# Sixteen small read-back transfers per scan step, issued by ScalarE instead of SyncE

## The chip, the cores and the metric

One core of one Trainium2 chip runs the whole program. The metric is the device time in microseconds (us) from the first to the last instruction of the core. One program computes two transformer-like blocks one after the other; the change is in one stage of the first block, the scan, which takes from about 624 us to 1393 us of the profiled execution.

## The reference, cut to what matters

The scan stage computes a linear recurrence over a 64x64 state per head, for 8 heads, in two directions (forwards and backwards), over 256 context tokens and then 1024 sequence tokens:

```python
def wkv_scan(state0, r, decay, kk, b, v, k, reverse):
    def step(S, inp):
        r_t, w_t, kk_t, b_t, v_t, k_t = inp
        sa = jnp.einsum("bhvk,bhk->bhv", S, kk_t)
        S = (S * w_t[:, :, None, :] - sa[..., None] * b_t[:, :, None, :]
             + v_t[..., None] * k_t[:, :, None, :])
        return S, jnp.einsum("bhvk,bhk->bhv", S, r_t)
    ...
    S, ys = lax.scan(step, state0, xs, reverse=reverse)
```

Everything else (projections, convolution, feed-forward block, two kinds of attention) runs before or after the scan and is not touched.

## The kernel before, in words

**Chunks.** The recurrence is done in chunks of 64 tokens: 4 chunks of context and 16 of sequence make `STEPS` = 20 steps, and each step handles one chunk of both directions x = 0 and x = 1, with all 8 heads held as 4 pairs. Within a chunk, the rank-one updates need the inverse of a 64x64 triangular matrix per head. It is put together from the inverses of its two 32x32 diagonal blocks: `level_y` and `last_u` on TensorE join them into the full inverse `uend`.

**The block inverses.** VectorE computes the 32x32 inverses for four steps at a time (`BATCH` = 4), spread over 128 partitions, in three parts that lie at the ends of steps s with s % 4 = 0, 1, 2 (`blocks(T, part)`). Part 2 ends with the semaphore `ui`. GpSimd then writes a transposed copy (`turned`, semaphore `ti`), and SyncE stores both to DRAM (`store_blocks`, semaphores `ub` and `tb`). From DRAM they come back in the layout of a step: `load_inverse(u)` waits, for the first step of a batch, until both stores have landed, and issues sixteen transfers of 16 KB (two directions x two heads of a pair x two blocks x two tensors `ud` and `td`), which raise the semaphore `inv`. `level_y(u)` on TensorE waits for it.

**The order of the queues.** Each engine's order is written out by hand. In step s:

- SyncE (the DMA queue SP): `load_inverse(s + 2)` unless s + 2 starts a batch; the stores of `raw` (s % 4 < 2, until step 9); the load of `nb` for the next batch of inverses (steps 1, 5, 9), which waits for part 1 of VectorE (`w_last`); the loads of `pre` (s % 4 >= 2, until step 7); then `load(x, s + 2)` for both directions, six transfers each (`rk`, `vc`, `kbk` and `vd` twice), which wait for the last reader of the buffers, `p_y` of the same direction (`p_s` in the first four steps); then the stores of `yo` to `ys`; and in steps with s % 4 = 2 `store_blocks` and then `load_inverse(s + 2)`.
- TensorE: `token_major(s + 1)` (line 1035, the transposes, which wait for the loads of step s + 1), `chain_g`, `triangles` l (bank 0, after ScalarE has copied `bet` out of it), `chain_z`, `triangles` m, `chain_s`, `level_y(s + 1)`, `chain_y`, `last_u(s + 1)`. Nearly all of it is in the helper `heads`, line 1005.
- ScalarE (helper `copy`, line 1136): four copies `c_bk` of `token_major(s + 1)`, two `c_gg`, two `c_zc`, the four half copies `c_zd`, where there are blocks the copies `c_raw`, and two `c_yo`, in this order.

So an engine that waits holds up everything behind it in this list. In the traces below the lines of the transfers are 889 to 894 (`load`), 900 (`load_pre`), 912 (`store_raw`), 921 (`load_blocks`), 925 and 927 (`store_blocks`), 942 and 944 (`load_inverse`) and 967 (`ys`).

Of the kernel before, what the change touches and what calls it, by code (L numbers as in the profile page):

```python
# [25 lines left out]
HEAD = 64  # L26
CH = 512
PAIRS = CH // P
# [5 lines left out]
STEPS = NCTX + NSEQ  # L34
# [788 lines left out]
def scan(nc, d, t):  # L823

    DIRS, HEADS = range(2), range(2)
    ROWS = [slice(HEAD * h, HEAD * h + HEAD) for h in HEADS]
    LOADS = 6 * 16
    BATCH = 4
    NBATCH = STEPS // BATCH
    HB = C // 2  # L830
    with ExitStack() as st:
# [46 lines left out]
        @block.sync  # L878
        def _(sp):
            def wait(name, x, value):  # L880
                if value > 0:
                    sp.wait_ge(S(name, x), value)

            def load(x, s):
                par, slot = s % 2, slot_of(x, s)
                ld_ = S(f"loaded{par}_", x)
                at = slice(slot * C, slot * C + C)
                part = lambda a0, a1, rows: d["ops"][x, a0:a1, :, rows, at].rearrange("a q p c -> p (a q) c")
                sp.dma_start(rk[x][par][:].rearrange("p a q c -> p (a q) c"), part(0, 2, slice(0, P))).then_inc(ld_, 16)
                sp.dma_start(vc[x][par][:], d["vts"][slot]).then_inc(ld_, 16)  # L890
                for h, rows in enumerate(ROWS):
                    sp.dma_start(kbk[x][par][rows, :, :, h].rearrange("p a q c -> p (a q) c"),
                                 part(1, 4, rows)).then_inc(ld_, 16)
                    sp.dma_start(vd[x][par][rows, :, h], d["vts"][slot, rows]).then_inc(ld_, 16)

            def load_pre(i):
                for x in DIRS:
                    wait("p_pre", x, i - 1)
                    slot = min(slot_of(x, 2 * i), slot_of(x, 2 * i + 1))
                    sp.dma_start(pre[x][i % 2][:].rearrange("p a q c -> p (a q) c"),  # L900
                                 d["ops"][x, 1:3, :, :, slot * C:(slot + 2) * C].rearrange("a q p c -> p (a q) c")
                                 ).then_inc(S(f"pre{i % 2}_", x), 16)

            def store_raw(i):

                for x in DIRS:
                    wait("raw", x, i + 1)
                    for h in HEADS:
                        for b in range(2):
                            rows = slice(HEAD * h + HB * b, HEAD * h + HB * (b + 1))  # L910
                            n = i % 2 * 2 * PAIRS
                            sp.dma_start(d["pb"][i // 2, x, h, b, n:n + 2 * PAIRS].rearrange("n r c -> r n c"),
                                         raw[x][i % 2][rows, :, :, HB * b:HB * (b + 1)].rearrange("p j q c -> p (j q) c")
                                         ).then_inc(sem(f"pb{i % 2}"), 16)

            def load_blocks(T):
                for j in range(2):
                    sp.wait_ge(sem(f"pb{j}"), 128 * (T + 1))
                if T:
                    sp.wait_ge(sem("w_last"), T)  # L920
                sp.dma_start(nb[:, 0:HB * HB], d["pb"][T].rearrange("x h b n r c -> (x h b n) (r c)")).then_inc(sem("nb"), 16)

            def store_blocks(T):
                sp.wait_ge(sem("ui"), T + 1)
                sp.dma_start(d["ub"][T].rearrange("x h b n r c -> (x h b n) (r c)"), ui[:, 0:HB * HB]).then_inc(sem("ub"), 16)
                sp.wait_ge(sem("ti"), T + 1)
                sp.dma_start(d["tb"][T].rearrange("x h b n r c -> (x h b n) (r c)"), ti[:].rearrange("p r c -> p (r c)")).then_inc(sem("tb"), 16)

            def load_inverse(u):
                T, par = u // BATCH, u % 2  # L930
                if u % BATCH == 0:
                    sp.wait_ge(sem("ub"), 16 * (T + 1))
                    sp.wait_ge(sem("tb"), 16 * (T + 1))
                for x in DIRS:
                    wait("uend", x, u - 1)
                    j = u % BATCH if x == 0 else u % BATCH // 2 * 2 + 1 - u % 2
                    of_u, of_t = (d["ub"], d["tb"]) if x == 0 else (d["tb"], d["ub"])
                    for h in HEADS:
                        for b in range(2):
                            rows, at = slice(HEAD * h + HB * b, HEAD * h + HB * (b + 1)), slice(HB * b, HB * (b + 1))  # L940
                            n = slice(PAIRS * j, PAIRS * (j + 1))
                            sp.dma_start(ud[x][par][rows, :, h, at], of_u[T, x, h, b, n].rearrange("n r c -> r n c")
                                         ).then_inc(S(f"inv{par}_", x), 16)
                            sp.dma_start(td[x][par][rows, :, at], of_t[T, x, h, b, n].rearrange("n r c -> r n c")
                                         ).then_inc(S(f"inv{par}_", x), 16)

            def step(s):
                if s + 2 < STEPS and (s + 2) % BATCH:
                    load_inverse(s + 2)
                if has_pre(s):  # L950
                    store_raw(pre_at(s))
                if s % BATCH == 1 and s // BATCH + 2 < NBATCH:
                    load_blocks(s // BATCH + 2)
                if s % BATCH >= 2 and s // BATCH + 3 < NBATCH:
                    load_pre(2 * (s // BATCH + 3) + s % BATCH - 2)
                for x in DIRS:
                    if s + 2 < STEPS:

                        if has_y(s):
                            wait("p_y", x, s + 1 - NCTX)  # L960
                        else:
                            wait("p_s", x, s + 1)
                        load(x, s + 2)
                for x in DIRS if has_y(s) else ():
                    wait("yo", x, s + 1 - NCTX)
                    at = slot_of(x, s) * C
                    sp.dma_start(d["ys"][x, :, :, at:at + C].rearrange("q p c -> p q c"),
                                 yo[x][s % 2][:]).then_inc(S(f"stored{s % 2}_", x), 16)
                if s % BATCH == 2 and s + 2 < STEPS:
                    store_blocks((s + 2) // BATCH)  # L970
                    load_inverse(s + 2)

            for i in range(2):
                load_pre(i)
            for par in range(2):
                for x in DIRS:
                    sp.wait_ge(sem("zeros"), 2 * par + x + 1)
                    load(x, par)
            for i in range(2):
                store_raw(i)  # L980
            load_pre(2)
            load_blocks(0)
            load_pre(3)
            for i in (2, 3):
                store_raw(i)
            load_pre(4)
            load_pre(5)
            load_blocks(1)
            sp.wait_ge(sem("clear"), 1)
            store_blocks(0)  # L990
            load_inverse(0)
            load_inverse(1)
            for s in range(STEPS):
                step(s)
            for x in DIRS:
                for par in range(2):
                    sp.wait_ge(S(f"stored{par}_", x), 16 * (NSEQ // 2))
# [132 lines left out]
        def _(act):  # L1130
# [4 lines left out]
            def copy(out, src, scale=1.0):  # L1135
                return nc.scalar.activation(out, src, ACT.Copy, scale=scale)

            def blocks(x, i):
                wait("p_pre", x, i + 1)
                if i >= 2:  # L1140
                    act.wait_ge(sem(f"pb{i % 2}"), 128 * (i // 2))
                copy(raw[x][i % 2][:].rearrange("p j q c -> p (j q c)"), bank[x][3][:]).then_inc(S("raw", x), 1)
# [33 lines left out]
            for i in (2, 3):  # L1176
                for x in DIRS:
                    blocks(x, i)
            for s in range(STEPS):
                if s + 1 < STEPS:  # L1180
                    token_major(s + 1)
                for x in DIRS:
                    chain_g(x, s)
                for x in DIRS:
                    chain_z(x, s)
                if has_y(s):
                    for x in DIRS:
                        chain_zd(x, s)
                if has_pre(s):
                    for x in DIRS:  # L1190
                        blocks(x, pre_at(s))
                if has_y(s):
                    for x in DIRS:
                        chain_y(x, s)

        @block.vector
        def _(dve):
# [1617 lines left out]
```

## Time and profile before

| what | value |
|---|---|
| median of 3 runs | 3318.89 us (3318.15 to 3340.68) |
| the profiled execution's own time | 3321.0 us |
| its span, first to last instruction | 3319.2 us |
| PE, DVE, ACT, POOL busy in the span | 2753.3, 1478.0, 812.2, 618.1 us |
| granted TensorE clock, share of full speed | 0.88 |
| scan, 624 to 1393 us: PE busy | 556.4 of 769 us |
| scan: granted clock, DMA share | 0.79, 0.37 |

PE is TensorE, DVE is VectorE, ACT is ScalarE, POOL is GpSimd; SPq and ACTq are the DMA queues of SyncE and ScalarE. The clock is a mean over the stretch. The DMA share is the mean busy share of the core's 16 DMA engines. Durations of an issue (SPq, ACTq) are the time that the issuing engine spends on it, not the transfer's.

### The profile page before, as it was taken

How to read it: one execution, taken by the hardware profiler on the slowest of the kernel's cores; microseconds unless marked ns; L12 is line 12 of the kernel's file. 1: busy time of each engine (PE TensorE's matmuls, PEld its weight loads, DVE VectorE, ACT ScalarE, POOL GpSimd, SP SyncE). 2: the span in 40 equal slices, each digit the busy share in tenths (PEclk: the TensorE clock that was granted, in tenths of full speed). 3: DMA queues.
4: the chain of work that ended last, by engine and by line, in shares of the span. 5: the costliest groups of instructions: out<-in, count | busy, mean ns of one | idle time of the engine just before them, and what ended most of it. 6: DMA issues, size and time to landing. Idle time of an engine off the chain costs nothing. (4 is left out here: it accounts for less than half of the span.)

```text
span 3319.2 us, 41107 instructions
## 1 busy us (share of the span) xinstructions
PE 2753.3 (83%) x14544; PEld 2303.8 (69%) x14544; DVE 1478.0 (45%) x1936; ACT 812.2 (24%) x1147; POOL 618.1 (19%) x302
## 2 busy tenths in 40 slices
PE   7788889747767888778799999697959898998879
PEld 6666668646766788756678888486747777776757
DVE  3166661254344353263466666402163554545251
ACT  1233321011111111133232333212232232223120
POOL 0334331000110101131222222233232011000001
PEclk8898888767878788889899999799979999998879
DMA  4233333433342424330111211423112101100022
GB/s 188 68 126 131 132 121 108 134 93 83 78 109 64 99 55 102 106 126 25 51 61 72 76 73 60 169 100 128 63 48 90 45 13 44 44 32 1 6 113 96
DMA packets 305065, 276.40 MB, mean 83 GB/s; under 512 B 228920, under 2 KB 264376, under 8 KB 293824
## 3 DMA queue, kind: packets, MB, share of 16 engines
q1 hardware_dynamic: 302656, 258.18, 24.3%
q10 hardware_dynamic: 2304, 16.78, 1.5%
q8 instruction: 70, 1.15, 0.1%
q14 instruction: 35, 0.29, 0.0%
HBM read 209.86 MB, written 65.04 MB: 83 GB/s over the span
## 5 line engine op out<-in xcount | busy, mean ns | idle before, releaser
L106 PE MATMUL e_ps<-h_hi,e_w_hi 128*128 128x512 f32 x704 | 276.6, 393 | 31.0 <-POOL e_w_lo L1935 30.2
L1959 DVE SCALAR_TENSOR_TENSOR e_acc<-e_grid,vec,e_acc 128x1024 f32<-128x1024 f32 x176 | 266.2, 1512 | 42.8 <-DVE e_acc L1959 37.4
L106 PE MATMUL e_ps<-h_hi,e_w_lo 128*128 128x512 f32 x704 | 274.8, 390 | 0.0
L106 PE MATMUL e_ps<-h_lo,e_w_hi 128*128 128x512 f32 x704 | 274.7, 390 | 0.0
L106 PE MATMUL b_ps<-h_hi,b_w_hi 128*128 128x512 f32 (+1 forms) x488 | 202.1, 414 | 39.1 <-POOL b_w_lo L651 31.6
L1035 PE MATMUL c_ps<-con,c_kbk 128*128 128x128 f32 x320 | 69.6, 390 | 153.4 <-DMA c_vd<-vts 153.4
L106 PE MATMUL b_ps<-h_lo,b_w_hi 128*128 128x512 f32 (+1 forms) x488 | 194.5, 399 | 0.0
L106 PE MATMUL b_ps<-h_hi,b_w_lo 128*128 128x512 f32 (+1 forms) x488 | 193.4, 396 | 0.0
L2063 PE MATMUL f_ps<-f_z_hi,f_w_hi 128*128 128x512 f32 x352 | 141.7, 403 | 49.2 <-DVE f_z_lo L2111 40.3
L1935 POOL TENSOR_TENSOR e_w_lo<-raw_up,e_w_hi 128x1024 fp32r<-128x1024 f32 x44 | 108.1, 2457 | 380.2 <-ACT e_w_hi L1906 380.2
L106 PEld LDWEIGHTS e_ps<-h_hi,e_w_hi 128*128 128x128 f32 x704 | 132.6, 188 | 66.1 <-issue 39.2
L1035 PEld LDWEIGHTS c_ps<-con,c_kbk 128*128 128x128 f32 x320 | 56.6, 204 | 162.3 <-DMA c_vd<-vts 162.3
L2419 POOL TENSOR_TENSOR g_w_lo<-raw,g_w_hi 128x1024 fp32r<-128x1024 f32 x32 | 76.6, 2406 | 474.9 <-ACT g_w_hi L2337 474.9
L106 PE MATMUL g_pb<-h_hi,g_w_hi 128*128 128x512 f32 x352 | 144.7, 411 | 9.7 <-issue 6.5
L106 PEld LDWEIGHTS b_ps<-h_hi,b_w_hi 128*128 128x128 f32 x488 | 100.2, 205 | 75.6 <-issue 56.6
L106 PEld LDWEIGHTS e_ps<-h_hi,e_w_lo 128*128 128x128 f32 x704 | 132.6, 188 | 27.9
L106 PEld LDWEIGHTS e_ps<-h_lo,e_w_hi 128*128 128x128 f32 x704 | 132.7, 189 | 27.0
L2265 PE MATMUL g_ps<-g_vt,g_pt 128*128 128x64 f32 x864 | 122.3, 292 | 30.1 <-DVE g_ot L2513 23.5
L1375 POOL TENSOR_SCALAR c_sd<-c_sc,con 128x256 f32<-128x256 f32 x64 | 58.4, 924 | 461.3 <-PE c_ps L1005 450.4
L106 PE MATMUL g_pb<-h_lo,g_w_hi 128*128 128x512 f32 x352 | 141.7, 402 | 0.0
L106 PE MATMUL g_pb<-h_hi,g_w_lo 128*128 128x512 f32 x352 | 141.6, 402 | 0.0
L2265 PEld LDWEIGHTS g_ps<-g_vt,g_pt 128*128 128x128 f32 x864 | 116.4, 211 | 36.2 <-issue 36.0
(320 smaller groups left out, 6232.7 us busy)
## 6 DMA issues: line engine op xcount, KB each, us to landing
raw_up<-w_ffn SPq DMA_DIRECT2D x22, 1024.0 KB, 4.9
raw_down<-w_down SPq DMA_DIRECT2D x16, 1408.0 KB, 6.1
b_adaw<-ada ACTq DMA_DIRECT2D x16, 1024.0 KB, 4.9
ops<-b_ops SPq DMA_DIRECT2D x16, 1024.0 KB, 4.5
raw<-w SPq DMA_DIRECT2D x8, 2048.0 KB, 7.6
c_kbk<-ops SPq DMA_DIRECT2D x80, 192.0 KB, 3.3
raw_in<-w SPq DMA_DIRECT2D x26, 512.0 KB, 3.8
zs<-e_z SPq DMA_DIRECT2D x22, 512.0 KB, 2.6
```

What stands on the lines that cost most here:

```text
L106: last = nc.tensor.matmul(out, w[:, k, :], x[:, k, cols], start=(k == 0 and n == 0), stop=(k == nk - 1 and n == 2))
L1035: mm = nc.tensor.transpose(bank[x][a][:, P * q:P * (q + 1)], kbk[x][par][:, 1 + a, q].rearrange("p h c -> p (h c)"), t["c_ident"])
L1375: a = TS(sd[x][:, :, h], sc[x][:], t["c_headones"][:, HEAD * h:HEAD * h + 1], None, ALU.mult)
L1935: nc.gpsimd.tensor_tensor(w_lo[:, s], raw[:, s], w_hi[:, s].bitcast(F32), ALU.subtract).then_inc(sem(f"lo{s}"), 1)
L1959: a = nc.vector.scalar_tensor_tensor(out=acc[:], in0=view, scalar=wt, in1=acc[:], op0=ALU.mult, op1=ALU.add)
L2063: mm = nc.tensor.matmul(ps[s][:], w[:, s, k], y[:, k], start=(k == 0 and n == 0), stop=(k == NFF - 1 and n == 2))
L2265: mm = nc.tensor.matmul(ps[0][:, 0:HEAD], pt[:, u % 2, b], vt[:, b, HEAD * h:HEAD * (h + 1)], start=(b == 0), stop=(b == qt))
L2419: nc.gpsimd.tensor_tensor(w_lo[:, tl], raw[:, tl], w_hi[:, tl].bitcast(F32), ALU.subtract).then_inc(sem(f"lo{tl}"), 1)
```

## The change: what it does

`load_inverse` moves from SyncE to ScalarE, unchanged in its waits, its transfers and its semaphores. ScalarE calls it for steps 0 and 1 ahead of its loop, and for step s + 2 as the last thing of its step s, behind the copies `c_yo`. SyncE keeps all the rest, `store_blocks` too.

```diff
@@ SyncE @@
-            def load_inverse(u):
-                T, par = u // BATCH, u % 2
-                if u % BATCH == 0:
-                    sp.wait_ge(sem("ub"), 16 * (T + 1))
-                    sp.wait_ge(sem("tb"), 16 * (T + 1))
...
             def step(s):
-                if s + 2 < STEPS and (s + 2) % BATCH:
-                    load_inverse(s + 2)
                 if has_pre(s):
                     store_raw(pre_at(s))
...
                 if s % BATCH == 2 and s + 2 < STEPS:
                     store_blocks((s + 2) // BATCH)
-                    load_inverse(s + 2)
...
             store_blocks(0)
-            load_inverse(0)
-            load_inverse(1)
             for s in range(STEPS):
                 step(s)
@@ ScalarE @@
+            def load_inverse(u):
+                T, par = u // BATCH, u % 2
+                if u % BATCH == 0:
+                    act.wait_ge(sem("ub"), 16 * (T + 1))
+                    act.wait_ge(sem("tb"), 16 * (T + 1))
+                for x in DIRS:
+                    wait("uend", x, u - 1)
+                    j = u % BATCH if x == 0 else u % BATCH // 2 * 2 + 1 - u % 2
+                    of_u, of_t = (d["ub"], d["tb"]) if x == 0 else (d["tb"], d["ub"])
+                    for h in HEADS:
+                        for b in range(2):
+                            rows, at = slice(HEAD * h + HB * b, HEAD * h + HB * (b + 1)), slice(HB * b, HB * (b + 1))
+                            n = slice(PAIRS * j, PAIRS * (j + 1))
+                            nc.scalar.dma_start(ud[x][par][rows, :, h, at], of_u[T, x, h, b, n].rearrange("n r c -> r n c")
+                                         ).then_inc(S(f"inv{par}_", x), 16)
+                            nc.scalar.dma_start(td[x][par][rows, :, at], of_t[T, x, h, b, n].rearrange("n r c -> r n c")
+                                         ).then_inc(S(f"inv{par}_", x), 16)
...
+            act.wait_ge(sem("clear"), 1)
+            load_inverse(0)
+            load_inverse(1)
             for s in range(STEPS):
                 if s + 1 < STEPS:
                     token_major(s + 1)
...
                 if has_y(s):
                     for x in DIRS:
                         chain_y(x, s)
+                if s + 2 < STEPS:
+                    load_inverse(s + 2)
```

## Rows read from the trace of the kernel before

**Rows 1.** Groups of instructions, 637 to 1393 us: busy, mean ns | idle before, releaser

```profile
L1035 PE MATMUL c_ps<-con,c_kbk 128*128 128x128 f32 x320 | 69.6, 390 | 153.4 <-DMA c_vd<-vts 153.4
```

**Rows 2.** Timeline of SyncE's queue, step 16: start us, duration us, what

```profile
1297.15 0.43 SPq L944 DMA_DIRECT2D c_td<-ub  x1
1309.50 0.39 SPq L889 DMA_DIRECT2D c_rk<-ops  x1
1316.72 0.65 SPq L894 DMA_DIRECT2D c_vd<-vts  x1
```

**Rows 3.** Timeline of ScalarE, steps 16 and 17, the last column is idle before

```profile
1298.78 0.38 ACT L1136 ACTIVATE c_zc<-c_ps 128x256 f32<-128x256 f32 x1 [2.30 <-PE c_ps L1005]
1309.50 0.38 ACT L1136 ACTIVATE c_yo<-c_ps 128x256 f32<-128x256 f32 x1 [7.71 <-PE c_ps L1005]
1312.18 0.38 ACT L1136 ACTIVATE c_yo<-c_ps 128x256 f32<-128x256 f32 x1 [2.30 <-PE c_ps L1005]
1320.78 0.60 ACT L1136 ACTIVATE c_bk<-c_ps 128x512 f32<-128x512 f32 x1 [3.76 <-PE c_ps L1035]
1324.65 0.38 ACT L1136 ACTIVATE c_gg<-c_ps 128x256 f32<-128x256 f32 x1 [1.56 <-PE c_ps L1005]
1329.11 0.38 ACT L1136 ACTIVATE c_zc<-c_ps 128x256 f32<-128x256 f32 x1 [2.30 <-PE c_ps L1005]
```

**Rows 4.** Stretches: us, engines' busy time (count), granted clock, DMA share, GB/s

```profile
1311.40:1319.40 8.00, 3.24 (x27) 2.81 (x26) 1.37 (x2) 0.98 (x2) 1.88 (x3) 1.00 0.96 229
1128.00:1133.00 5.00, 5.00 (x47) 5.00 (x46) 2.80 (x6) 2.05 (x5) 0.00 (x0) 1.00 0.23 34
```

**Rows 5.** Timeline of SyncE's queue, steps 6 and 7

```profile
973.18 0.32 SPq L942 DMA_DIRECT2D c_ud<-ub  x1
...
981.34 0.44 SPq L942 DMA_DIRECT2D c_ud<-ub  x1
...
990.03 1.02 SPq L889 DMA_DIRECT2D c_rk<-ops  x1
```

**Rows 6.** Timeline of ScalarE, steps 6 to 8

```profile
956.85 0.38 ACT L1136 ACTIVATE c_yo<-c_ps 128x256 f32<-128x256 f32 x1 [2.30 <-PE c_ps L1005]
...
974.38 0.38 ACT L1136 ACTIVATE c_zc<-c_ps 128x256 f32<-128x256 f32 x1 [2.30 <-PE c_ps L1005]
...
1003.49 0.60 ACT L1136 ACTIVATE c_bk<-c_ps 128x512 f32<-128x512 f32 x1 [3.82 <-PE c_ps L1035]
```

**Rows 7.** Timeline of TensorE, step 7: triangles l, then chain_z

```profile
971.50 2.00 PE L1005 MATMUL c_ps<-c_rk,c_kbk 128*128 128x128 f32 x16
973.34 1.90 PE L1005 MATMUL c_ps<-c_gg,c_uend 128*128 128x64 f32 x16
```

**Rows 8.** Timeline of SyncE's queue, step 3: first transfer of the batch's second step

```profile
830.99 0.43 SPq L942 DMA_DIRECT2D c_ud<-ub  x1
```

**Rows 9.** Timeline of ScalarE, steps 2 to 4

```profile
786.73 0.60 ACT L1136 ACTIVATE c_bk<-c_ps 128x512 f32<-128x512 f32 x1 [3.17 <-PE c_ps L1035]
...
799.07 0.38 ACT L1136 ACTIVATE c_zc<-c_ps 128x256 f32<-128x256 f32 x1 [3.52 <-PE c_ps L1005]
...
814.35 1.09 ACT L1136 ACTIVATE c_bk<-c_ps 128x512 f32<-128x512 f32 x2 [3.30 <-PE c_ps L1035]
...
826.31 0.38 ACT L1136 ACTIVATE c_zc<-c_ps 128x256 f32<-128x256 f32 x1 [3.58 <-PE c_ps L1005]
...
852.99 0.60 ACT L1136 ACTIVATE c_bk<-c_ps 128x512 f32<-128x512 f32 x1 [3.47 <-PE c_ps L1035]
```

**Rows 10.** Stretches, as rows 4, each just after a long wait of TensorE

```profile
787.00:800.00 13.00, 13.00 (x73) 13.00 (x72) 2.04 (x4) 2.71 (x7) 0.00 (x0) 0.59 0.15 45
935.00:943.00 8.00, 8.00 (x63) 8.00 (x62) 1.29 (x3) 2.56 (x5) 0.00 (x0) 0.84 0.36 108
```

**Rows 11.** Timeline of both DMA queues, 498 us, an issue on each at once

```profile
498.18 0.34 SPq L334 DMA_DIRECT2D mixd<-b_r  x1
498.42 0.34 ACTq L547 DMA_DIRECT2D b_adaw<-ada  x1
```

More of the change, by code:

```diff
@@ L927, in store_blocks @@
                 sp.dma_start(d["tb"][T].rearrange("x h b n r c -> (x h b n) (r c)"), ti[:].rearrange("p r c -> p (r c)")).then_inc(sem("tb"), 16)
-            def load_inverse(u):
-                T, par = u // BATCH, u % 2
-                if u % BATCH == 0:
-                    sp.wait_ge(sem("ub"), 16 * (T + 1))
-                    sp.wait_ge(sem("tb"), 16 * (T + 1))
[L934 to L945, printed above, removed]
             def step(s):
-                if s + 2 < STEPS and (s + 2) % BATCH:
-                    load_inverse(s + 2)
                 if has_pre(s):
```

## The prediction

> **What bounds the kernel now.** I read the groups of instructions of the scan first: which group is TensorE idle in front of? It is the transposes on line 1035, which open a step, with 153.4 us of idle time released by the loads of the step's inputs [rows 1]. So every scan step is a chain through SyncE's queue, and the next view is that queue's timeline in an ordinary step, beside ScalarE's. In step 16 the last of the sixteen inverse transfers is issued at 1297.15, and then the queue is idle until the loads start at 1309.50 [rows 2], the moment in which ScalarE is also released by the same `p_y` [rows 3]. The sixteen issues are therefore finished 12 us before the loads become possible: **in an ordinary step they delay nothing where they are**. The twelve loads are issued until 1316.72 + 0.65 = 1317.37 [rows 2], and the second direction's `c_bk` copy runs at 1320.78 [rows 3]. Third, the stretches: from 1311.4 to 1319.4 the DMA engines are 0.96 busy [rows 4], so in that window the transfers themselves are the limit, not only their issue.
>
> The exception is the turn of a batch (steps 2, 6, 10 and 14 and the step after each). There the queue waits for the stores, issues 32 inverse transfers (973.18 on, the second sixteen from 981.34) and only then, at 990.03, the loads [rows 5]. That step is long.
>
> **What goes.** The time from direction 0's `c_zc` to direction 1's next `c_bk` is 1320.78 - 1298.78 = 22.0 in the ordinary step [rows 3]. At the turn it is 1003.49 - 974.38 = 29.1 [rows 6]. With the queue free and the first batch of transfers landed early this falls to the ordinary length: 7.1 us less, in each of three turns of this pattern (6, 10, 14). In the first turn the steps have no output: 852.99 - 826.31 = 26.7 against the preceding step's 814.35 - 799.07 = 15.3 [rows 9], 11.4 less. Together 3 x 7.1 + 11.4 = **-32.7**.
>
> **What comes, first: ScalarE stalls at the turns.** ScalarE's last copy of step 6 ends at 957.23 [rows 6]. Behind it now stand the waits for both stores, which let SyncE go at 973.18, and sixteen issues, 973.18 to 981.34 = 8.2 us with SyncE's own durations [rows 5]; an issue alone costs ScalarE's queue the same as SyncE's, 0.34 [rows 11]. SyncE has issued that step's loads before, so nothing disturbs this batch. Queued behind it on ScalarE are the four `c_bk` and the `c_gg` copies of step 7; TensorE waits for them in `triangles` and `chain_z`. From 981.34: four copies of 0.60 [rows 3] are 2.4, `c_gg` 0.38, then from `chain_z`'s start to `c_zc` 974.38 - 973.34 = 1.04 [rows 6, 7]; the triangles, 973.34 - 971.50 = 1.84 [rows 7] after the first copy, fit beside that. So `c_zc` comes at 981.34 + 3.8 = 985.2 instead of 974.38: +10.8. In the first turn it is 830.99 + 3.8 = 834.8 instead of 826.31 [rows 8, 9]: +8.5. Together 3 x 10.8 + 8.5 = **+40.9**. `level_y` comes after that and finds its transfers landed. The POOL queue and `store_blocks` are passed by nothing: they stand where they were.
>
> **Second: ordinary steps, on ScalarE.** Its issues start when the second `c_yo` ends, 1312.18 + 0.38 = 1312.56, and take 8.2 at most: 1320.7. The first `c_bk` is late by that, but the second was only due at 1320.78 and the first `c_gg` at 1324.65 [rows 3]; four copies from 1320.7 end at 1323.1. Cost **0**; the cover is the wait for the loads itself, with 1.5 us to spare. Were the issues slower by more than that, each microsecond more would be paid in every step. In the first four steps, without `c_yo`, they start earlier still.
>
> **Third: ordinary steps, on the DMA engines.** Before, the sixteen transfers ran while the engines were idle; now they run from 1312.6 on, inside the full window. Alone they take 0.23 of the engines [rows 4] for some 8.2 x 0.23 = 1.9 us of their time; those issued before the last load lands are about four fifths, 1.5 us, and in a window that is full that much work pushes the last load back by as much. No row shows what the engines do between two queues. From below: 0, if the loads' backlog is served first. From above: the issues hinder each other (first rival), 3.5. I take 1.5, since the 0.96 row is the nearest. It counts in eleven steps: 18 have a `load_inverse`, less four turns, less steps 1, 5 and 9, in which SyncE still waits for VectorE when ScalarE has finished. 11 x 1.5 = **+16.5**.
>
> Here the Trainium skill speaks against the change. Its page "DMA: Bandwidth & Descriptors", section "Queues, rings and completion order", says that an engine takes turns between the queues that have work for it. By it the small transfers aren't held back behind the loads, and all sixteen count, 1.9 us in each step in place of 1.5: 4 us more in the sum. No row of before has both queues full, so the trace neither agrees nor disagrees.
>
> **Fourth: the clock.** A new wait of some 10 us in `triangles` (from about 971.5 to 982) comes at each turn. After long waits TensorE restarts at the lower clock: it was granted 0.59 over 13 us in one case and 0.84 over 8 us in another [rows 10]. At the low clock the way from `c_bk` to `c_zc` took 799.07 - 786.73 = 12.3 [rows 9], in step 17 1329.11 - 1320.78 = 8.3 [rows 3]: 4.0 dearer. Per turn 0 to 4, I take 2: 4 x 2 = **+8**. The eleven steps wait 1.5 us longer too; if one in ten of them falls to the long low stretch it is 11 x 0.4 = **+4.4** (0 to 11).
>
> **The sum.** -32.7 + 40.9 + 0 + 16.5 + 8 + 4.4 = +37.1. The profiled execution took 3321.0, 2.1 above the median of the runs shown; against it the sum gives 3358.1, against the median 3318.9 + 37.1 = **3356**. The transfers for steps 0 and 1, ahead of the loop, stand behind the same stores on either queue: nothing.
>
> **Rivals.**
> - *The issues of the two queues exclude each other.* After 1312.56 SyncE has 4.8 us of its twelve issues left, seven loads; if each lets one inverse issue through, 8.2 / 16 = 0.5, the last load goes 3.5 us later. That replaces the 1.5 (the backlog then drains meanwhile): 11 x 2.0 = +22, so 3378. For it: issues back to back take longer than one alone (0.65 against 0.39 [rows 2]), so something behind the queue is occupied. Against: two issues that overlapped by 0.1 us took 0.34 each [rows 11], but both were alone in their queue. The Trainium skill, "Perfetto Trace Analysis", section "DMA Instruction — HWDGE (DVE, Sync)", says that the descriptor generator is locked for one issue at a time; by that rule this rival holds.
> - *The loads aren't disturbed.* SyncE's backlog is served first, both clock terms small: -32.7 + 40.9 = +8.2, plus at most 5, so 3327 to 3332. For it: five loads are issued before ScalarE starts. Against: the 0.96.
> - *Faster, by the turns.* The price of the stall is decided in ScalarE's step after a turn: if its copies didn't have to wait for the end of the issues (the stores early, or the step's copies already done), only -32.7 + 16.5 remains, 3303, and 3286 without the disturbance as well. It decides from a stall under 7.1 us per turn. Against: ScalarE would have to be released by 977.6 instead of 981.34, and its first issue can't start before 973.18.
> - *It doesn't do what it says*: nothing is reordered by the change beyond these queues; a gain or loss within 3 us either way would need all four terms to cancel.
>
> **How the numbers follow.** About 1%, 33 us, is what a measurement of this kernel tells from no change, so the limits are 3286 and 3352. Forecast case 0.50, lying at 3340 to 3372 by the clock and the stall's length, so six tenths of it above 3352; exclusion 0.25 (3365 to 3395); undisturbed 0.17; faster 0.05, half of it past 3286; no effect 0.03. Slower 0.30 + 0.25 = 0.55 and a little of the third's upper end, 0.57; faster 0.03; the same 0.40. The range takes the undisturbed case and the bulk of the exclusion: 3326 to 3390.
>
> **What would show it.** ScalarE idle from about 957 to 973 at the turn and its sixteen issues behind, TensorE waiting some 10 us before `triangles` l there, released by `c_bk`; the turn's second half 7 us shorter, with the loads issued at `p_y`; in ordinary steps `p_y` to the second direction's transposes 1.5 us longer, the DMA share near 1.0 over a longer stretch, and SyncE's issues of 0.65 as they were (in the first rival they grow to over 1 us). Wrong if ScalarE's issues cost over 0.6 each, if the loads land no later, or if TensorE's clock in the scan moves from 0.79 by more than 0.03.

## The result, and the profile after

After: 3348.54 us median of 19 runs (3332.84 to 3367.23). Before, on the same chip: 3318.15 (19 runs, 3301.34 to 3340.68). The ratio is 1.0096, 95% interval 1.0075 to 1.0117: some 30 us slower, at the limit of 1%. The forecast was +37.

The profiled execution of after took 3332.84 us, the lowest of the 19, so its span is only 12 us longer than before's. From direction 0's `c_zc` of step 0 to that of step 19, though, it is 676.5 us against 659.5: +17.0. Ahead of it +5.5 and behind it -10.6 are work that the change doesn't touch (5.3 of the 5.5 are there already at the last `c_raw` copy before the scan steps, 673.72 against 668.43, and TensorE's wait for the two batches ahead of the loop is the same, 34.4 against 34.5 us).

In after, `heads` is line 982 (1005 before), the transposes 1012 (1035), ScalarE's copy 1113 (1136), the moved transfers 1128 and 1130 (942, 944). From the page: busy time by engine, the clock by slice, the queues (packets, MB, share).

```profile
PE 2722.4 (82%) x14544; PEld 2273.1 (68%) x14544; DVE 1475.9 (44%) x1936; ACT 809.9 (24%) x1147; POOL 629.1 (19%) x302
PEclk8798888867878788979899999899979999999989
q1 hardware_dynamic: 256576, 252.92, 23.2%
q10 hardware_dynamic: 48384, 22.04, 2.5%
```

ScalarE's queue q10 now carries the transfers (2304 packets before, 48384 now). Work and clock did not become worse in this execution: PE is busy 30.9 us less, at 0.885 of full speed against 0.880. The loss is waiting. Where, the groups of the scan show (637 to 1410 us; columns as in [rows 1]):

```profile
L982 PE MATMUL c_ps<-c_rk,c_kbk 128*128 128x128 f32 x640 | 88.5, 297 | 43.0 <-ACT c_bk L1113 43.0
L1012 PE MATMUL c_ps<-con,c_kbk 128*128 128x128 f32 x320 | 70.8, 396 | 154.3 <-DMA c_vd<-vts 154.3
L1113 ACT ACTIVATE c_bk<-c_ps 128x512 f32<-128x512 f32 x80 | 45.6, 598 | 341.8 <-issue 180.8 <-PE c_ps L1012 160.9
```

The wait for the loads is as in [rows 1] (154.3, 153.4). New is the first line: `triangles` waits 43.0 us for `c_bk`, and waited 0.0 before. The third says why `c_bk` is late: for over half of the idle time before it ScalarE waited for nothing that is computed ("issue"), but was with its own queue. At a turn, where [rows 6] stood, ScalarE's timeline of steps 6 to 8 is:

```profile
962.17 0.38 ACT L1113 ACTIVATE c_yo<-c_ps 128x256 f32<-128x256 f32 x1 [2.30 <-PE c_ps L982]
979.29 0.31 ACTq L1128 DMA_DIRECT2D c_ud<-ub  x1
...
986.40 0.45 ACTq L1130 DMA_DIRECT2D c_td<-ub  x1
986.90 2.06 ACT L1113 ACTIVATE c_bk<-c_ps 128x512 f32<-128x512 f32 x4 [24.35 <-issue]
...
991.90 0.38 ACT L1113 ACTIVATE c_zc<-c_ps 128x256 f32<-128x256 f32 x1 [2.39 <-PE c_ps L982]
...
1014.29 1.71 ACT L1113 ACTIVATE c_bk<-c_ps 128x512 f32<-128x512 f32 x3 [8.61 <-issue]
```

Four `c_bk` back to back are a pile that waited: 24.35 us idle, which end with the last of sixteen issues. TensorE, transposes and then `triangles` l and `chain_z` of step 7 [rows 7]:

```profile
970.34 2.82 PE L1012 MATMUL c_ps<-con,c_kbk 128*128 128x128 f32 x12 [3.98 <-DMA c_vd<-vts]
...
987.55 3.48 PE L982 MATMUL c_ps<-c_rk,c_kbk 128*128 128x128 f32 x16 [10.65 <-ACT c_bk L1113]
990.86 1.90 PE L982 MATMUL c_ps<-c_gg,c_uend 128*128 128x64 f32 x16
```

And SyncE's queue, which at 981.34 was in the middle of 32 issues [rows 5], is idle until `p_y` releases its loads:

```profile
973.84 0.33 SPq L925 DMA_DIRECT2D ub<-c_ui  x1
975.84 0.33 SPq L927 DMA_DIRECT2D tb<-c_ti  x1
976.21 1.47 SPq L900 DMA_DIRECT2D c_pre<-ops  x2
1002.62 0.37 SPq L889 DMA_DIRECT2D c_rk<-ops  x1
```

In an ordinary step, 15 to 16, first SyncE, then ScalarE, then TensorE, where [rows 2, 3] stood:

```profile
1299.42 0.38 SPq L889 DMA_DIRECT2D c_rk<-ops  x1
...
1301.83 0.98 SPq L892 DMA_DIRECT2D c_kbk<-ops  x1
...
1307.04 0.65 SPq L894 DMA_DIRECT2D c_vd<-vts  x1
```

```profile
1302.11 0.39 ACT L1113 ACTIVATE c_yo<-c_ps 128x256 f32<-128x256 f32 x1 [2.29 <-PE c_ps L982]
1302.12 0.33 ACTq L1128 DMA_DIRECT2D c_ud<-ub  x1
...
1310.56 0.45 ACTq L1130 DMA_DIRECT2D c_td<-ub  x1
1311.06 0.60 ACT L1113 ACTIVATE c_bk<-c_ps 128x512 f32<-128x512 f32 x1 [8.56 <-issue]
1311.83 0.60 ACT L1113 ACTIVATE c_bk<-c_ps 128x512 f32<-128x512 f32 x1 [0.17 <-PE c_ps L1012]
...
1315.96 0.38 ACT L1113 ACTIVATE c_gg<-c_ps 128x256 f32<-128x256 f32 x1 [1.83 <-PE c_ps L982]
```

```profile
1310.67 2.82 PE L1012 MATMUL c_ps<-con,c_kbk 128*128 128x128 f32 x12 [3.88 <-DMA c_vd<-vts]
```

The second `c_bk` is released by PE, not by "issue": ScalarE was ready 0.17 us before it was needed.

The ledger, from the `c_zc` of direction 0 in the two traces (us; a turn is two steps; `c_yo` is that of direction 0 in the step before):

| turn | length before | after | `c_yo` to `c_zc` before, after | `c_zc` to 2nd `c_bk` before, after |
|---|---|---|---|---|
| steps 3, 4 | 62.3 | 65.2 | (step length 27.24, 38.89) | 26.7, 17.9 |
| 7, 8 | 68.3 | 74.5 | 20.2, 32.4 | 29.1, 22.9 |
| 11, 12 | 70.6 | 74.8 | 20.1, 32.1 | 27.0, 23.3 |
| 15, 16 | 65.7 | 74.5 | 20.0, 32.0 | 27.9, 23.1 |

The first halves cost 11.6 + 12.2 + 12.0 + 12.0 = 47.9 (from the unrounded lengths), the second give back 8.8 + 6.2 + 3.8 + 4.7 = 23.5. The turns together are 22.1 longer; in before, step 12 had a low-clock stretch between its `c_bk` and `c_zc` (below), so it is some 26 with that set aside.

What the second half gives back has two sources, and only one is SyncE's shorter queue. In before, TensorE also waits at the turns inside `level_y`, for direction 1's transfers, and each time a stretch at the low clock follows (0.50 to 0.53 of full speed). In step 15 of before, then the same place in step 7 of after, where `c_zc` is so late that all sixteen have landed:

```profile
1272.72 1.94 PE L1005 MATMUL c_ps<-c_td,c_ld 128*128 128x64 f32 x8 [1.76 <-DMA c_td<-ub]
1273.00:1279.00 6.00, 6.00 (x30) 6.00 (x29) 0.69 (x1) 0.00 (x0) 0.00 (x0) 0.50 0.23 35
```

```profile
997.96 1.95 PE L982 MATMUL c_ps<-c_td,c_ld 128*128 128x64 f32 x16
```

From `c_zc` to the next `c_yo` before took 13.1, 14.6 and 16.0 us in steps 7, 11 and 15; after takes 10.7 each time, 11.5 less together. In steps 11 and 15 that is the whole give-back: from `c_yo` to the second `c_bk` of the next step it is 12.4 and 11.9 us before, 12.5 and 12.4 after. Only step 7 (16.1 to 12.2) and the first turn, which has no `c_yo`, are shorter by the loads.

### The profile page after: what moved, and what is told of

It reads as the page before. It is cut to its first block and busy times, and to the rows that moved or that the text cites. A ratio compares the mean times of both kernels' runs of the same rounds, so it can differ in the third digit from the quotient of the medians.

```text
span 3331.1 us, 41107 instructions
## 1 busy us (share of the span) xinstructions
PE 2722.4 (82%) x14544; PEld 2273.1 (68%) x14544; DVE 1475.9 (44%) x1936; ACT 809.9 (24%) x1147; POOL 629.1 (19%) x302
## 3 DMA queue, kind: packets, MB, share of 16 engines
q10 hardware_dynamic: 48384, 22.04, 2.5%
## 5 line engine op out<-in xcount | busy, mean ns | idle before, releaser
L106 PE MATMUL e_ps<-h_hi,e_w_hi 128*128 128x512 f32 x704 | 275.7, 392 | 32.4 <-POOL e_w_lo L1935 32.4
L1959 DVE SCALAR_TENSOR_TENSOR e_acc<-e_grid,vec,e_acc 128x1024 f32<-128x1024 f32 x176 | 264.2, 1501 | 42.8 <-DVE e_acc L1959 37.4
L1012 PE MATMUL c_ps<-con,c_kbk 128*128 128x128 f32 x320 | 70.8, 396 | 154.3 <-DMA c_vd<-vts 154.3
L1935 POOL TENSOR_TENSOR e_w_lo<-raw_up,e_w_hi 128x1024 fp32r<-128x1024 f32 x44 | 118.8, 2700 | 368.4 <-ACT e_w_hi L1906 368.4
L106 PEld LDWEIGHTS e_ps<-h_hi,e_w_hi 128*128 128x128 f32 x704 | 132.7, 188 | 65.3 <-issue 37.1
L2265 PE MATMUL g_ps<-g_vt,g_pt 128*128 128x64 f32 x864 | 114.6, 280 | 32.2 <-DVE g_ot L2513 25.8
L2063 PE MATMUL f_ps<-f_z_lo,f_w_hi 128*128 128x512 f32 x352 | 140.5, 399 | 0.0
```

The costliest lines, as they stand in the source:

```text
L106: last = nc.tensor.matmul(out, w[:, k, :], x[:, k, cols], start=(k == 0 and n == 0), stop=(k == nk - 1 and n == 2))
L1012: mm = nc.tensor.transpose(bank[x][a][:, P * q:P * (q + 1)], kbk[x][par][:, 1 + a, q].rearrange("p h c -> p (h c)"), t["c_ident"])
L1935: nc.gpsimd.tensor_tensor(w_lo[:, s], raw[:, s], w_hi[:, s].bitcast(F32), ALU.subtract).then_inc(sem(f"lo{s}"), 1)
L1959: a = nc.vector.scalar_tensor_tensor(out=acc[:], in0=view, scalar=wt, in1=acc[:], op0=ALU.mult, op1=ALU.add)
L2063: mm = nc.tensor.matmul(ps[s][:], w[:, s, k], y[:, k], start=(k == 0 and n == 0), stop=(k == NFF - 1 and n == 2))
L2265: mm = nc.tensor.matmul(ps[0][:, 0:HEAD], pt[:, u % 2, b], vt[:, b, HEAD * h:HEAD * (h + 1)], start=(b == 0), stop=(b == qt))
```

## The experiments

All ratios are against runs of the kernel before on the same chip. The diffs are against after or before as said. In `e1_turns`, `e2_ordinary`, `e4_mid` and `e5_second` one engine issues the first batch of four steps and the other the second, so the second waits for both stores as well (`u % BATCH < 2` in place of `== 0`); the diffs leave this line and the copied `load_inverse` out.

**Where the loss sits: turns alone, the rest alone.** `e1_turns`, against after: ScalarE issues only the batches that open four steps; SyncE issues all others where it did before.

```diff
 (ScalarE)
-                if s + 2 < STEPS:
+                if s + 2 < STEPS and (s + 2) % BATCH == 0:
                     load_inverse(s + 2)
 (SyncE)
+                if s + 2 < STEPS and (s + 2) % BATCH:
+                    load_inverse(s + 2)
```

> ScalarE issues only the four batches that open a turn (steps 4, 8, 12 and 16), at the end of its step; all others stay on SyncE. Theory (the loss is ScalarE's stall at the turns, some 12 us each, less what SyncE's shorter queue gives back there): most of the loss is still there, 15 to 25 us over the kernel before, ratio 1.005 to 1.008, and from direction 0's c_yo to the next second c_bk in ordinary steps it is 11.8 as before, not 12.5. Rival (the loss is the clash with the loads in ordinary steps): within 5 us of the kernel before.

Measured: 3348.34 us, 1.0073 (1.0048 to 1.0098). `c_yo` to `c_zc` at the turns is 31.9 to 32.4, as in after; the second transposes of steps 9, 13, 14, 17 and 18 start 10.7 us after `c_yo`, near before's 10.6. `e2_ordinary` is the reverse (SyncE keeps the opening batches, ScalarE issues all others at the end of its step).

> The reverse: SyncE keeps the four batches that open a turn, ScalarE issues all others at the end of its step. Theory: no stall at the turns (c_bk at its old place, 4 us after c_yo), so the kernel is no slower than the one before: +8 us for the clash in eleven steps (0.7 each), -10 to -20 at the turns because SyncE issues 16 instead of 32 before the loads; ratio 0.996 to 1.001. Rival (clash in ordinary steps carries the loss): +15 us or more, ratio 1.005 or over.

Measured: 3320.73 us, 0.9986 (0.9964 to 1.0008). No loss. So the loss is made where ScalarE waits for the stores and issues sixteen in one go; what the other fourteen batches cost and what they give back at the turns come out even here. 1.0096 - 1.0073 = 0.0023, 8 us, is what they add in after, if the difference of two ratios, each uncertain by as much, is taken at its word.

**What of the stall is the wait, what the issues.** `e8_wait`, against before: ScalarE only waits, and issues nothing.

```diff
+                if s % BATCH == 2 and s + 2 < STEPS:
+                    act.wait_ge(sem("ub"), 16 * ((s + 2) // BATCH + 1))
+                    act.wait_ge(sem("tb"), 16 * ((s + 2) // BATCH + 1))
```

> The kernel before, all transfers on SyncE, but ScalarE also waits for both stores at the end of steps 2, 6, 10 and 14. It pays the wait and not the sixteen issues. Theory: the stall in the changed kernel is the wait (some 4 us beyond its cover) and the issues (7.6 us), one after the other; here only the first: direction 0's c_zc 24 to 25 us after the preceding c_yo instead of 20.1 (changed kernel: 32.1), and a part of it hidden since level_y waits for its transfers anyway; +6 to +14 us over the kernel before. Rival (the wait alone makes the loss): as slow as the kernel with the turns on ScalarE, +25.

Measured: 3319.99 us, 1.0017 (0.9998 to 1.0035), by the ratio 5.6 us and just under the 6 to 14 expected. ScalarE at the turn:

```profile
973.86 2.06 ACT L1136 ACTIVATE c_bk<-c_ps 128x512 f32<-128x512 f32 x4 [15.97 <-DMA tb<-c_ti]
...
978.85 0.38 ACT L1136 ACTIVATE c_zc<-c_ps 128x256 f32<-128x256 f32 x1 [2.38 <-PE c_ps L1005]
```

`c_zc` comes 3.8 us late (24.0 after `c_yo`, against 20.2), but steps 7 and 8 together take 68.5 us, as before (68.3). What comes behind was waiting for SyncE anyway and now waits less: `c_yo` of step 7 to the second `c_bk` of step 8 is 13.1 us (16.1 before), and `c_zc` to `c_yo` in steps 11 and 15 is 10.8 and 12.8 (14.6 and 16.0). The issues behind the wait are what costs.

`e10_half`, against before: ScalarE issues only direction 1's eight transfers of the opening batch at the end of its step; SyncE keeps direction 0's.

```diff
-            def load_inverse(u):
+            def load_inverse(u, dirs=DIRS):
...
-                for x in DIRS:
+                for x in dirs:
 (SyncE, s % BATCH == 2)
-                    load_inverse(s + 2)
+                    load_inverse(s + 2, (0,))
 (ScalarE, end of the step)
+                if s % BATCH == 2 and s + 2 < STEPS:
+                    load_inverse(s + 2, (1,))
```

> The kernel before, but of the batch that opens a turn ScalarE issues direction 1's eight transfers, at the end of steps 2, 6, 10 and 14; direction 0's eight and all else stay on SyncE. The stall now holds eight issues. Theory (the stall lengthens by each issue, 0.48 us): the preceding c_yo to direction 0's c_zc is 28 us at the turns, between 24.0 with none and 32.1 with sixteen; 5 to 15 us over the kernel before. Rival (what follows the wait is paid once, not per issue): 32.

Measured: 3338.63 us, 1.0042 (1.0016 to 1.0067). `c_yo` to `c_zc` is 28.6, 28.7 and 28.9 at the three turns. With the wait alone, eight issues and sixteen it is 24.0, 28.7 and 32.2: 4.7 for the first eight, 3.5 for the next. The stall grows with the number of issues ahead of `c_bk`.

**The price of one issue.** `e3_tiny`, against after: each of the moved transfers brings one partition instead of 32, so the step's inverses are incomplete.

```diff
-    nc.scalar.dma_start(ud[x][par][rows, :, h, at], of_u[T, x, h, b, n].rearrange("n r c -> r n c")
+    nc.scalar.dma_start(ud[x][par][rows.start:rows.start + 1, :, h, at], of_u[T, x, h, b, n, 0:1].rearrange("n r c -> r n c")
```

> The changed kernel with the same sixteen issues, each carrying one of its 32 partitions (so the inverses are mostly left out and the output is not the reference's). If the 0.7 us by which loads land later in ordinary steps is the DMA engines' work, it goes: c_yo to second c_bk back to 11.8, time 5 to 10 us under the changed kernel's 3348. If the two queues' issues exclude each other it stays at 12.5, and SyncE's load issues stay as long as in the changed kernel. The stall at the turns stays in both.

Measured: 3368.97 us, 1.0131 (1.0092 to 1.017): slower, against expectation. The bytes of a transfer fell to a thirty-second, but its issue became dearer:

```profile
981.14 0.56 ACTq L1128 DMA_DIRECT2D c_ud<-ub  x1
...
989.97 0.56 ACTq L1130 DMA_DIRECT2D c_td<-ub  x1
990.58 2.06 ACT L1113 ACTIVATE c_bk<-c_ps 128x512 f32<-128x512 f32 x4 [26.10 <-issue]
```

0.56 us each against 0.45 makes 9.4 us for sixteen, 1.8 more, and the way from there to `c_zc` is longer too: `c_yo` to `c_zc` at the turns is 34.5 to 35 us. The turn steps 3, 7, 11 and 15 are 1.0, 2.5, 2.4 and 2.7 us longer than in after, 8.7 together, most of the 0.0035 between the two ratios: the loss grows with the time of an issue, not with the bytes. In the ordinary steps ScalarE is busy until 12.5 us after `c_yo` (11.7 in after), later than its second `c_bk` is wanted, and still nothing is paid in the steps at the high clock: steps 13, 14 and 18 take 31.40, 30.61 and 31.11 us, in after 31.50, 30.70 and 31.23, for the first `c_gg` is on time (15.42 us after `c_yo` in step 14, 15.52 in after). The cover is the time to the first `c_gg`, as the prediction had it, and not to the second `c_bk`. (Steps 8, 16 and 17 of this run fell into low-clock stretches and those of after didn't; such stretches vary by as much in one kernel, see `e6_again`, so that this has to do with the longer burst is not shown.) The second transposes start at 10.8 us after `c_yo` on the mean of steps 9, 13, 14, 17 and 18 (11.1 in after, 10.6 before). The run was meant to isolate the clash on the DMA engines through `c_bk`, and `c_bk` here is set by ScalarE: for that it was the wrong measure.

**The rest of the gain, without the loss.** `e4_mid`, against before: SyncE keeps the opening batches, ScalarE issues all others in the middle of its step, ahead of the `c_yo` copies.

```diff
 (SyncE)
-                if s + 2 < STEPS and (s + 2) % BATCH:
-                    load_inverse(s + 2)
 (ScalarE, ahead of chain_y)
+                if s + 2 < STEPS and (s + 2) % BATCH:
+                    load_inverse(s + 2)
```

> SyncE keeps the batches that open a turn; ScalarE issues the others, but ahead of its c_yo copies instead of behind, where it has 7.7 us to wait anyway and the DMA engines are idle. Theory: neither stall nor clash: ordinary steps as before (11.8), turns 3 to 9 us shorter since the loads no longer wait behind the second sixteen transfers: 15 to 20 us faster than the kernel before, ratio 0.994 to 0.996. Rival (issues on ScalarE cost whatever their place): not faster than the kernel with them at the end.

Measured: 3319.05 us, 0.9989 (0.9967 to 1.0012). Missed. The loads aren't disturbed (second transposes at 10.4 to 11.1 us in steps 13, 14, 17 and 18), and the turns are shorter (steps 3 and 4 together 55.9 us, 7 and 8 65.0; 62.3 and 68.3 before). In the steps with `c_raw` copies the issues start late and hold up `c_yo`, here in step 8 to 16.1 us after `c_zc` from 12.9:

```profile
1024.99 0.60 ACT L1134 ACTIVATE c_raw<-c_ps 128x512 f32<-128x512 f32 x1 [0.34 <-PE c_ps L1024]
1024.99 0.36 ACTq L1149 DMA_DIRECT2D c_ud<-ub  x1
...
1032.21 0.51 ACTq L1151 DMA_DIRECT2D c_td<-ub  x1
1032.82 0.66 ACT L1134 ACTIVATE c_yo<-c_ps 128x256 f32<-128x256 f32 x2 [7.23 <-issue]
```

But the loads wait for TensorE's `p_y` and not for this copy, and `c_yo` to the next second `c_bk` is shorter by about as much (9.3 us after step 8, 11.8 before). So this delay costs 1 us or so each time and doesn't explain the missing 10 to 15 us. What isn't gained sits in `level_y`: it still waits at the turns, since SyncE still issues all sixteen in a row, here in step 15:

```profile
1267.51 1.94 PE L1003 MATMUL c_ps<-c_td,c_ld 128*128 128x64 f32 x8 [1.80 <-DMA c_td<-ub]
```

`c_zc` to `c_yo` takes 15.0, 12.1 and 16.0 us in steps 7, 11 and 15, together as long as in before (13.1, 14.6, 16.0) and 10.9 longer than with the 10.7 of after. The low clock from `c_bk` to `c_zc` in step 16, here and not in before, hides some more in this one trace (steps 15 and 16 take 71.1 against 65.7 us).

`e5_second` moves only the batches of u % 4 == 1, which at a turn stand ahead of SyncE's loads, to that place on ScalarE; `e7_behind` leaves them on SyncE, behind the loads:

```diff
-                if s + 2 < STEPS and (s + 2) % BATCH:
+                if s + 2 < STEPS and (s + 2) % BATCH > 1:
                     load_inverse(s + 2)
...
                         load(x, s + 2)
+                if s + 2 < STEPS and (s + 2) % BATCH == 1:
+                    load_inverse(s + 2)
```

> The kernel before, with only the second batch of each turn (steps 5, 9, 13 and 17) on ScalarE, ahead of its c_yo copies in the step before, where it waits 7.7 us anyway; everything else stays on SyncE. Theory: this takes what the change gives (loads no longer behind 32 issues at the turns: the first direction's c_yo to the second c_bk 16.0 to 12 in step 8, and c_zc to c_bk 26.7 to 20 in step 4) and none of what it costs: 8 to 14 us faster than the kernel before, ratio 0.996 to 0.998. Rival (the loads at the turns are limited by something else): no difference.

> The kernel before, with the second batch of each turn still on SyncE but issued behind the loads of its step instead of ahead of them. Theory: the same gain as with that batch on ScalarE, 8 to 14 us, ratio 0.996 to 0.998, with no issue on ScalarE at all: what the change gives comes from the order in SyncE's queue, not from a second queue. Rival (a second queue is needed): no difference from the kernel before.

Measured: 3304.75 us, 0.9977 (0.9955 to 0.9999), and 3311.19 us, 0.9991 (0.9968 to 1.0013). In both the loads' wait in the turn's second half falls (step 8, `c_yo` to second `c_bk`: 16.05 before, 12.58 and 12.09; in step 4 26.7 from `c_zc`, then 19.4 and 19.0). The gain is small, for the second not told from none. One reason is again `level_y`: direction 1's transfers are where they were, it waits 0.6 to 1.8 us for them at each of the three turns, and in step 7 `c_zc` to `c_yo` grows to 14.0 and 15.7 us (13.1 before).

**The opening batch, half of it behind `c_zc`.** `e9_split`, against before: as `e10_half`, but ScalarE issues its eight in the next step, behind the copies `c_zc`.

```diff
+                if s % BATCH == 3 and s + 1 < STEPS:
+                    load_inverse(s + 1, (1,))
```

> The same eight transfers on ScalarE, but placed behind its c_zc copies of the next step, when both stores have landed and the c_bk and c_gg copies are done. Theory: no stall (c_zc 20 us after c_yo as before); both directions' transfers are issued side by side and land 3 us or so earlier, so level_y no longer waits (c_zc to c_yo 10.7 to 12 at the turns, 13 to 16 before), and SyncE is through with its 24 issues before the loads are due: 10 to 20 us faster than the kernel before, ratio 0.994 to 0.997. Rival: a wait elsewhere takes it back, no difference.

Measured: 3306.15 us, 0.9955 (0.9936 to 0.9974). ScalarE at the turn:

```profile
982.69 0.60 ACT L1136 ACTIVATE c_bk<-c_ps 128x512 f32<-128x512 f32 x1 [4.16 <-PE c_ps L1035]
...
991.54 0.39 ACT L1136 ACTIVATE c_zc<-c_ps 128x256 f32<-128x256 f32 x1 [0.51 <-PE c_ps L1005]
991.62 0.35 ACTq L1151 DMA_DIRECT2D c_ud<-tb  x1
...
996.05 0.48 ACTq L1153 DMA_DIRECT2D c_td<-ub  x1
996.63 1.71 ACT L1136 ACTIVATE c_zd<-c_zc 64x256 f32<-64x256 f32 x4 [4.71 <-issue]
```

`c_bk` runs when PE releases it and `c_zc` comes 20.7, 20.1 and 19.9 us after `c_yo`, as before. And `level_y` gets its transfers sooner: ScalarE begins direction 1's 1.0 us after `c_zc`, while SyncE is still at direction 0's, and ends 4.7 us after it (5.9 in step 7), where SyncE alone ended at 6.4 to 7.3. TensorE waits 0.7 us there in step 7 and not at all in steps 11 and 15: `c_zc` to `c_yo` is 11.6, 10.7 and 10.7 us. Against `e10_half` the same eight issues stand one stretch later: 0.9955 against 1.0042, 29 us, for their place alone.

**Both.** `e11_both` is `e9_split` and `e7_behind` together, and `e12_again` is the same kernel once more.

> The kernel before with two edits together. (a) Of the sixteen transfers that open a batch, SyncE issues direction 0's eight at the turn and ScalarE direction 1's eight behind the copies c_zc of the next step, as in e9_split. (b) The transfers of the batch's second step are issued by SyncE behind that step's loads instead of ahead of them, as in e7_behind. Theory (a turn is SyncE's work: whatever stands ahead of the loads lengthens it, and ScalarE's work costs only where a copy waits behind it): e9_split has already taken 0.0045 of the time, and left 24 transfers ahead of the loads of the second step; its step 4 still has 22.95 us from the preceding step's c_zc to the second c_bk against 18.96 in e7_behind, its step 8 13.55 against 12.09, steps 12 and 16 11.73 and 12.50, which is the ordinary length. So only some 4 + 1.5 us are left: 3298 to 3303 us, ratio 0.992 to 0.996, step 4 near 19 us, step 8 near 12, steps 12 and 16 unchanged. Rival (the two edits take away the same microseconds, or the transfers behind the loads come late for level_y of the batch's second step): no better than e9_split, 0.9955 to 0.998.

> The kernel of e11_both once more, unchanged, with more rounds: its four runs gave 0.9895 with an interval of 0.985 to 0.994, below the 0.992 to 0.996 expected. In its trace the turns have the length forecast (steps 3 and 4 together 52.1 us against 62.3 before, steps 11 and 12 62.0 against 70.6, steps 15 and 16 61.7 against 65.7), and two of its four executions came out at 3283.6, 19 below the others, which is five steps' worth of long low-clock stretches at some 4 us each. Theory (the turns give 18 to 23 us, the rest of the 28 was a lucky draw of the clock): ratio 0.991 to 0.995, median 3296 to 3303. Rival (shorter turns also lead to fewer low-clock restarts, a gain that the turns' lengths do not show): 0.987 to 0.991, with at most two steps whose way from the second c_bk to c_zc is 12 us.

Measured: 3292.85 us, 0.9895 (0.9849 to 0.9942), and 3296.06 us, 0.9917 (0.9884 to 0.9949): 27 to 35 us under before by the ratios, the fastest version of this study. SyncE at the turn (`e11_both`):

```profile
970.26 0.32 SPq L942 DMA_DIRECT2D c_ud<-ub  x1
...
973.95 1.06 SPq L900 DMA_DIRECT2D c_pre<-ops  x2
986.57 0.37 SPq L889 DMA_DIRECT2D c_rk<-ops  x1
...
994.73 0.65 SPq L894 DMA_DIRECT2D c_vd<-vts  x1
995.42 0.60 SPq L942 DMA_DIRECT2D c_ud<-ub  x1
```

Eight issues at the turn, then idle until the loads are possible, the second batch behind them. Steps 11 and 12 take 62.0 us (70.6 before), 15 and 16 61.7 (65.7), 3 and 4 52.1 (62.3). Steps 7 and 8 gain nothing (70.3, and 68.1 in `e12_again`; 68.3 before): there `level_y` still waits, 2.3 and 2.5 us, and `c_zc` to `c_yo` takes 15.3 and 16.7. Why at this turn alone was not isolated. In `e12_again` three steps have a low-clock stretch, so the rival's "at most two" isn't met, and 0.9917 fits the theory's range and not quite the rival's; its interval covers both.

**The kernel after once more.** `e6_again` is after, unchanged.

> The changed kernel once more, for a second trace. If the 12 us by which the first profiled span was longer than before understate the change because TensorE fell into the long low-clock stretch in 1 step of the scan against 5 before, this trace has 3 to 6 such steps and a span of 3340 to 3355; the turns (two steps each) are 4 to 9 us longer than before again. If the turns don't carry the loss, their lengths change with the span.

Measured: 3354.25 us, 1.0108 (1.0076 to 1.014), span of the profiled execution 3371.0, above the 3340 to 3355 expected. The turn steps are the same as in the first trace (38.8, 43.3, 42.9, 43.2 us for steps 3, 7, 11, 15; 38.9, 43.1, 42.8, 42.7 there), the rest is not. Step 14 from the last `c_bk` on, first in `e6_again`, then in after (us, busy of PE, PEld, DVE, ACT, POOL, clock, DMA share, GB/s):

```profile
1262.60:1274.40 11.80, 11.80 (x66) 11.80 (x64) 3.84 (x5) 2.52 (x7) 0.00 (x0) 0.58 0.02 3
```

```profile
1238.40:1246.00 7.60, 7.60 (x65) 7.60 (x63) 3.71 (x5) 2.46 (x7) 0.00 (x0) 0.91 0.02 4
```

The same work, 4.2 us longer at 0.58. Of steps 1 to 18 such stretches between the last `c_bk` and `c_zc` fell on 8 in `e6_again` (2, 4, 5, 9, 12, 13, 14, 18; 3 to 6 were expected), on 1 in after (9), on 5 in before (2, 3, 9, 12, 13). Four stretches fewer, some 16 us, and the 5 us net outside the scan are why the profiled execution of after was only 12 us longer than before's, while the medians are 30 apart.

## Why the prediction was right

Its sign, its main mechanism (ScalarE's stall at the turns) and its range were right (+37.1 forecast, +30 measured, 3348.5 in 3326 to 3390). That the sum came so close is partly luck: what goes was taken 9 us too large and the clash on the DMA engines 11 too large, and the two cancel. Term by term:

- **The stall at the turns, +40.9, with the clock's +8.** Measured 47.9 for both (48.9 forecast). For step 7 the parts are: ScalarE's first issue 19.8 us after `c_yo`, where SyncE's was 19.0 (+0.8); sixteen issues in 7.6 us, not 8.2 (-0.6); from their end to `c_zc` 5.0 us, not 3.8 (+1.2), since `triangles` l took 3.48 us after its wait of 10.65, and 2.00 in [rows 7]. The granted clock was 0.56 from 987.5 to 991 us, right behind that wait. From the end of the issues to `c_zc` the four turns took 6.1, 5.1, 5.5 and 5.5 us, so the clock term was 2.3 in the first and 1.3 to 1.7 in the others, inside its 0 to 4. That the rows of the change are enough is shown by `e1_turns` (the loss with the turns alone) and `e2_ordinary` (none without them).
- **What goes, -32.7.** Mis-sized: 23.5. It took the 29.1 of step 7 [rows 6] for all three turns, but before's own trace has 27.0 and 27.9 at the other two, where no `pre` loads are issued; and it set the new length at an ordinary 22.0, which has become 22.9 to 23.3. The pattern should have been read at each turn. Its cause was half right too: it put the gain to SyncE's free queue and the early transfers in one, while half of it (11.5 us) is `level_y`'s wait and the low clock behind it, and that goes in after because `c_zc` comes 11 us or more late. This half is bought with the stall, and `e4_mid` and `e5_second`, which have no stall, don't get it; `e9_split` gets nearly all of it without the stall, by issuing direction 1's transfers sooner.
- **ScalarE in ordinary steps, 0.** Right. The burst there is 8.7 to 9.2 us, longer than the 8.2 assumed, and ends 11.4 to 11.9 us after `c_yo` where 11.2 was forecast, so it uses 0.2 to 0.7 of the 1.5 us named. `e3_tiny`, whose burst ends at 12.5, uses 1.3 of them and paid nothing in its steps at the high clock.
- **The clash on the DMA engines, +16.5.** Too large: the second transposes of steps 9, 13, 14, 17 and 18 start 11.10 us after `c_yo` on the mean, 10.59 before. 0.5 us, not 1.5; 11 x 0.5 = 5.5, and `e1_turns`, without it, is 8 us faster than after by the ratios (each uncertain by as much). By the lengths of steps 14, 17 and 18, all at the high clock, it is 0.2 a step (30.92 after, 30.72 before). The Trainium skill's rule in "DMA: Bandwidth & Descriptors", section "Queues, rings and completion order", by which an engine takes turns between the queues, would have made it 1.9; the trace has less. Why so little was not isolated.
- **The clock in ordinary steps, +4.4.** Not to be told from the variation of 1 to 8 such stretches in one and the same kernel.

With the measured sizes the sum is 26 for the turns plus 2 to 5.5, so 28 to 32, beside 30 measured. 24.4 of the 26 are 47.9 - 23.5; 1.5 more lie in step 16, whose way from the second `c_bk` to `c_zc` went from 7.07 to 8.60. That is the clock: the granted clock there was 1.00 in before (1291.0 to 1298.8 us) and 0.80 in after (1311.0 to 1320.4).

The rivals. **Exclusion of the issues** fell: SyncE's twelve load issues take 7.8 to 8.5 us in the ordinary steps of after, 7.7 to 8.4 before, and its issues of 0.61 to 0.65 stand unchanged beside ScalarE's, whose burst grew from 7.55 to 8.9 us. Clearest is `e1_turns`, where both engines issue sixteen of the small transfers in the same 7.6 us, each at the durations it has alone:

```profile
974.63 0.43 SPq L944 DMA_DIRECT2D c_td<-tb  x1
974.66 0.46 ACTq L1152 DMA_DIRECT2D c_td<-tb  x1
```

The Trainium skill describes a lock of the descriptor generator for one issue at a time ("Perfetto Trace Analysis", section "DMA Instruction — HWDGE (DVE, Sync)"). The trace doesn't bear out that it costs these two queues anything. **Undisturbed loads** had the small delay of the loads nearly right, but the turns alone cost more than its 3327 to 3332. **Faster by the turns** needed copies that don't wait for the issues; after hasn't that, and `e9_split` and `e11_both`, which have, are faster, as that rival said. **No effect** is excluded by the interval.

## What to carry to other kernels

An issue costs its engine's time at the place in its order where it stands: ask which instruction is queued behind it and who waits for that, and put it where the next instruction isn't wanted yet (here behind `c_zc`, not ahead of `c_bk`). Moving a queue's work to relieve one engine only pays if the burst, with the wait ahead of it, fits into idle time of the other; splitting it between both did. And a wait can hide behind a delay: after lost `level_y`'s wait only because it was late, so ask of each gain whether it outlives the repair of the loss. Where a pattern recurs, read its length at each recurrence before it is multiplied.

## What the runs showed of the hardware

- A transfer of one partition costs ScalarE more time to issue (0.56 us) than one of 32 partitions (0.45), back to back. Fewer bytes aren't a cheaper issue.
- Two queues issuing at once: sixteen issues of ScalarE take 7.55 us alone, 7.6 beside sixteen like ones of SyncE (`e1_turns`), and 8.7 to 9.2 beside SyncE's loads, while SyncE's take no longer (0.43 and 0.61 to 0.65 us each, as alone).
- A short wait can be followed by the low clock, and need not be: behind a wait of 0.66 us in `level_y` TensorE was granted 0.50 (before, 1136 to 1142 us), behind one of 1.16 us 1.00 (`e4_mid`, 1138 to 1141 us).
- The number of stretches that TensorE spends at the low clock (0.58 over 11.8 us, 3.7 to 4.2 us dearer than the same work at the high one) differs from 1 to 8 between executions of one kernel. Single profiled executions of this kernel can't settle 15 us; lengths of the same step at the same clock can settle one.
